# Sixteen unread identity products between the fourth and fifth tiles of the first projections

## The reference, cut to what matters

```
mod = silu(c) @ ada_w + ada_b
shift1, scale1, ... = split(mod)
h = rmsnorm(x, norm1_g) * (1 + scale1) + shift1
proj = h @ w_in
qa, ka, va, qb, kb, vb, ga, gb = split(proj)
... windowed attention on qa, ka, va; block attention on qb, kb, vb;
... gates, output projection, MLP, then a second block (convolution,
... feed-forward, forgetting attention, feed-forward)
```

## Time and profile before

| what | value |
|---|---|
| median of 3 runs | 1969.68 us (1968.35 to 1969.92) |
| the profiled execution's own time | 1967.05 us |
| its span, first to last instruction | 1965.3 us |
| PE busy | 1906.1 us, 97% of the span |
| DVE, ACT, POOL busy | 1180.5, 779.4, 343.6 us |
| mean granted clock of PE | 0.992 of full speed |

### The profile page before, as it was taken

One profiled execution on the slowest core, in us unless ns is written; L12 is line 12 of the kernel. 1 busy time (PEld: TensorE's weight loads), 2 busy tenths in 40 slices (PEclk: granted clock), 3 DMA queues, 4 the chain that ended last, 5 costly groups with the idle time before them and its releaser, 6 DMA issues.

```text
span 1965.3 us, 22312 instructions
## 1 busy us (share of the span) xinstructions
PE 1906.1 (97%) x8952; PEld 1577.2 (80%) x8952; DVE 1180.5 (60%) x1853; ACT 779.4 (40%) x1180; POOL 343.6 (17%) x307
## 2 busy tenths in 40 slices
PE   4999999999999999999999999999999999999997
PEld 3788888878888887888788888877898778888886
DVE  6687665576676745665655644476777754433446
ACT  4677622352223235222422222256677442222223
POOL 4323111021111112002300000036533130000003
PEclk9999999999999999999999999999999999999998
DMA  9522366266566434432545432313211223223221
GB/s 333 150 84 70 134 223 237 88 226 221 217 209 219 150 107 158 164 127 86 213 173 192 173 127 86 108 65 129 70 44 65 88 85 100 93 90 103 95 99 43
DMA packets 126232, 267.54 MB, mean 136 GB/s; under 512 B 4576, under 2 KB 33264, under 8 KB 126129
## 3 DMA queue, kind: packets, MB, share of 16 engines
q1 hardware_dynamic: 121168, 248.59, 37.0%
q0 software_dynamic: 4960, 17.53, 2.5%
HBM read 261.84 MB, written 8.45 MB: 138 GB/s over the span
## 4 chain that ended last, share of the span: by engine, by line
PE 70%; DVE 3%; ACT 2%; POOL 2%; issue 1%; DVEq 0%; POOLq 0%; ACTq 0%
PE ps L624 22%; PE ps L626 22%; PE ps L625 22%; PE ps L784 1%; PE ps L773 0%; ACT t L1212 0%; PE ps L762 0%; ACT t L1216 0%; POOL t L2316 0%; PE ps L801 0%; PE ps L802 0%; PE ps L800 0%; DVE t L1628 0%; DVE t L1613 0%; POOL t L2125 0%
## 5 line engine op out<-in xcount | busy, mean ns | idle before, releaser
L624 PE MATMUL ps<-t 128*128 128x512 f32 (+1 forms) x2504 | 966.7, 386 | 10.3 <-POOL t L2220 4.2
L626 PE MATMUL ps<-t 128*128 128x512 f32 (+1 forms) x2504 | 958.9, 383 | 0.0
L625 PE MATMUL ps<-t 128*128 128x512 f32 (+1 forms) x2504 | 955.0, 381 | 0.0
L1549 DVE TENSOR_TENSOR t<-t 128x2048 fp32r<-128x2048 f32 x133 | 305.4, 2296 | 440.4 <-ACT t L1163 440.2
L624 PEld LDWEIGHTS ps<-t 128*128 128x128 f32 x2504 | 470.7, 188 | 104.5 <-POOL t L2125 5.6
L626 PEld LDWEIGHTS ps<-t 128*128 128x128 f32 x2504 | 470.3, 188 | 96.4
L625 PEld LDWEIGHTS ps<-t 128*128 128x128 f32 x2504 | 470.5, 188 | 90.8 <-issue 1.0
L1163 ACT ACTIVATE t<-t 128x2048 fp32r<-128x2048 f32 x133 | 254.3, 1912 | 612.8 <-PE ps L626 605.3
L1613 DVE SCALAR_TENSOR_TENSOR t<-ps,t 128x512 f32<-128x512 f32 x184 | 131.7, 748 | 81.4 <-PE ps L626 78.0
L1561 DVE CUSTOM_DVE_ANT_0 t<-t 128x1024 f32<-128x1024 f32 x144 | 174.8, 1255 | 6.7 <-DMA t<-in_adakv_t 3.5
L2125 POOL TENSOR_TENSOR t<-t 128x512 fp32r<-128x512 f32 x88 | 115.5, 1332 | 196.8 <-ACT t L1170 196.2
(11 more groups left out here) (171 smaller groups left out, 1526.1 us busy)
## 6 DMA issues: line engine op xcount, KB each, us to landing
t<-in_ada SPq DMA_DIRECT2D x48, 1024.0 KB, 5.9
t<-in_gate SPq DMA_DIRECT2D x22, 1024.0 KB, 5.1
t<-in_up SPq DMA_DIRECT2D x22, 1024.0 KB, 5.1
t<-in_down SPq DMA_DIRECT2D x22, 1024.0 KB, 5.0
t<-in_w_in SPq DMA_DIRECT2D x17, 1024.0 KB, 5.7
t<-in_w_mlp_in SPq DMA_DIRECT2D x16, 1024.0 KB, 5.3
t<-in_w_mlp_out SPq DMA_DIRECT2D x16, 1024.0 KB, 5.0
t<-in_ada_t POOLq DMA_DIRECT2D x13, 1024.0 KB, 6.0
```

The costliest lines, as they stand in the source:

```text
L624: pe.matmul(o, wh, xh, start=first, stop=False)
L625: pe.matmul(o, wh, xl, start=False, stop=False)
L626: return pe.matmul(o, wl, xh, start=False, stop=last)
L1549: dve.tensor_tensor(WL[:, n % NW, :], raw[:, n % NRAW, :], WH[:, n % NW, :].bitcast(F), ALU.subtract).then_inc(w_lo_d.sem, w_lo_d.up("slot ...
```

## The change

Between the 24 matmuls of slot 1 on tiles 0 to 3 and the 12 of slot 0 on tiles 4 and 5, PE issues sixteen products of the identity with 256 columns of constants into bank 3. They wait for nothing new and signal nothing. Nothing is removed or moved.

```diff
-            for n, us in ((0, (0, 1)), (0, (2, 3)), (1, (0, 1, 2, 3)), (0, (4, 5)), (1, (4,)), (0, (6, 7)), (1, (5, 6, 7))):
+            for n, us in ((0, (0, 1)), (0, (2, 3)), (1, (0, 1, 2, 3)), (None, ()), (0, (4, 5)), (1, (4,)), (0, (6, 7)), (1, (5, 6, 7))):
+                if n is None:
+                    for _ in range(16):
+                        pe.matmul(psum[3][:, 0:256], ident, cst[:, 0:256], start=True, stop=True)
                 for u in us:
                     for i in range(2):
                         job_unit(f"qa{n}", n, i, u, QA_BANKS[n][i], "h1")
```

## The result

The changed kernel took 1975.6 us as the median of 5 runs (1974.59 to 1978.96), the kernel before 1969.18 us in the 5 runs beside it (1966.61 to 1969.92). The ratio is 1.0036 with a 95% interval of 1.0025 to 1.0048: 6.4 us slower as medians, 4.9 to 9.5 us by the interval. A second comparison, on another occasion, gave 1.0038 (1.0024 to 1.0052), which is 4.7 to 10.2 us, and 8.8 us as medians. The forecast was 1976.6 us, 6.9 us slower.

What follows compares the result with a forecast made beforehand. PE was taken to bound the kernel, busy 1906.1 us of a 1965.3 us span. Thirty-two added records at 0.216 us give 6.9 us, less 0 recovered: 1969.68 + 6.9 = 1976.6 us, range 1973.2 to 1978.8 us.

Steps and rivals of the forecast that it cites:

- The place holds no gap: Between slot 1 and tile 4: PE starts tile 4 at 50.06 us without a wait, so the products cannot be hidden.
- The price of a record: At the inserted products: 0.216 us each at full clock, 6.9 us for 32 records.
- entry and exit: Changes between `mm3` and plain float32 around the products: claimed to cost nothing visible, checked at L699.
- The rule of the Trainium skill: For the inserted records: 131 ns per 512-column matmul would give 4.2 us; the prediction set it aside for the trace.
- Nothing recovered behind it: Behind the products: later waits hang on PE and move with it, so 0 us recovered.
- The waits were to be the same within a microsecond: Sign in the profile after: PE's total waits unchanged within a microsecond, its busy time longer by 6.9 us.
- Rival C, half clock: At the inserted products: they run at half clock and cost 14.0 us, giving 1983.7 us; chance 0.03.
- Rival D, the narrow price: At the products: records cost only what narrow matmuls do, or partly vanish; 3.5 us, 1973.2 us; chance 0.03.
- Rival B, the drops at the norms: At later norms: all clock drops vanish, 3.2 us come back, leaving 3.7 us, 1973.4 us; chance 0.06.
- Rival E, faster: At the products: they keep the clock up and make the kernel faster; chance 0.01, with anything else making it faster.

Runs made afterwards that it cites:

- in_the_gap: The same 16 products placed ahead of tiles 2 and 3 on slot 0, added to the kernel before: ratio 0.9997 (0.9988 to 1.0006).
- wide_512: Sixteen plain float32 products of 512 columns in place of 256, at the changed kernel's place: ratio 1.007 (1.0055 to 1.0084) against the kernel before.
- halves_256: Sixteen fp32r products of 256 columns in place of the plain float32 ones, at the changed kernel's place: ratio 1.0003 (0.9994 to 1.0012) against the kernel before.
- gap_8: Eight of the products placed ahead of tiles 2 and 3 on slot 0, added to the kernel before: ratio 0.9994 (0.9985 to 1.0003).
- fill_4: Four of the products placed ahead of slot 1 on tiles 0 to 3, added to the kernel before: ratio 0.9998 (0.999 to 1.0007).

## Why the prediction was right

**The place holds no gap.** Right. In both profiles of the changed kernel PE steps from slot 1 into the products without a wait. Tile 4's low half was ready 1.05 us before PE came to it, so that without the products there was nothing to wait for either. The contrast is `in_the_gap`, where the same products cost nothing that can be told.

**The price of a record.** Right: 0.216 us forecast from the earlier trace rows, 0.216 us measured, for 32 and for 64 records. That entry and exit cost nothing visible was right in sum: the long first step behind them (56.38 to 56.80 us) takes the place of the last record's own step, and the total is 6.9 us, as L699 had shown. The rule of the Trainium skill weighed there, 131 ns a matmul of 512 columns in sustained streams (same page, section "Back-to-back issue gap"), has no counterpart in the records measured here: a record of 512 columns took 0.227 us in fp32r and 0.43 us in plain float32 (`wide_512`).

**Nothing recovered behind it.** Right. The delay at 1303 us is that at 930 us to 0.01 us. The wait for slot 2 stayed at 0.34 us, the waits at L784 at 5.1 against 4.7 us in total. The waits were to be the same within a microsecond and grew by 1.4 us, none having become shorter by more than 0.5 us, and PE's busy time grew by 6.6 us where 6.9 were forecast; the drops of the clock that differ between the two executions are in both numbers.

**Rival C, half clock.** Did not happen at this place in any profile (ahead of slot 1 the first products did run at half clock, 7.40 us for the 32 records instead of 7.07). But the prediction's reason, full clock from 46 us on the earlier trace rows, was that of one execution: in five of nine the window from 46 to 48 us is at 0.50, and the clock is back for good only shortly before the products begin. There the clock was back about 3 us ahead of the products rather than 6, so this part of the forecast held with less room than it says.

**Rival D, the narrow price.** Fell with `halves_256` and `wide_512`: 0.12 us is the price of an fp32r record of 256 columns. A plain record costs nearly twice that, and a plain call has two of them.

**Rival B, the drops at the norms.** Only a part of its mechanism exists. One drop of the earlier trace rows, of 2.0 us, was absent after, and one of 2.2 us came in elsewhere; this one comes and goes in the kernel before as well. The other two that the rival counted, 0.4 and 0.8 us, belong to drops that are in all fourteen profiles, so of the 3.2 us that it gives back the profiles bear out no more than the 2.0. That such drops widen the scatter of both kernels and move the difference of the medians by little is argued: it fits the ratios and was not measured by itself.

**Rival E, faster.** The change can't reach the early drops that it might prevent: in all profiles of kernels with this gap they are over before the products. Placed where products could prevent one (`in_the_gap`, `gap_8`, `fill_4`), they don't make the kernel measurably faster. Where only the first drop occurs, POOL's low half of slot 1 holds PE at 44.5 us with or without full clock. Where a second one would have come, up to 1.6 us could be saved, and the intervals of these ratios are too wide to show a mean of that size or less. No variant here beats the kernel before by more than can be told.

## What to carry to other kernels

Work that keeps an engine busy is free only as far as a wait of that engine, there or shortly behind, takes it up, and the wait has to be found in the timeline: the same sixteen products cost 6.9 us where PE has no wait and nothing that can be told ahead of tile 2. Price such a filler by records of the same form at the same clock, from start to start; a plain float32 call of 256 columns costs 0.43 us and an fp32r one 0.12 us. And before reading a few microseconds between two profiled executions as an effect, profile the kernel before again, more than once: here two of its own executions differ by 2.0 us at a single norm.

## What was unexpected of the hardware

- The clock of PE takes one of two courses behind the same idle time of 3.6 us. Either it is at 0.50 when the twelve matmuls begin and is back at about 44 us, or it falls within them, is back at 42 us, and falls again behind a wait of 1.75 us, to about 49 us. The second course costs 1.6 us in all, because there the low clock lies on the matmuls of slot 1; in the first it ends before them, and slot 1's matmuls start 6.4 us behind tile 2's in both.
- Over the four products of L897 in the kernel before (27 to 31 us) the view of windows prints a clock of 1.00, while their records are 0.63 us long and step by 0.43 us, twice the 0.38 and 0.216 us of the same records at full clock. So they ran at half clock, as the prediction read them, and the view's 1.00 is not to be trusted at the head of the span: the trace has no record of the clock ahead of 30.7 us.
- In the profile of `gap_8` an idle time of 3.27 us left the clock at 1.00.
- For plain float32 records of 128 columns PE goes on at 0.11 us a record although the profile gives each weight load a length of 0.19 us. The weight loads overlap each other in the profile (32 of them in 3.76 us), so their length is no lower bound for the spacing.
